# Four instead of three of eight units by seven products in the up and projection pairs

## What is computed

```python
h = h + 0.5 * swiglu(rms_norm(h, g1), w_gate1, w_up1, w_down1)      # FFN 1, inner width 5632
u = rms_norm(h, g_mix)
q, k, v, ... = split(u @ w_in)                                      # projection
merged = sigmoid(gate_A) * (attention(...) @ W_A) + sigmoid(gate_B) * (gla(...) @ W_B)
h = h + merged @ w_out
h = h + 0.5 * swiglu(rms_norm(h, g2), w_gate2, w_up2, w_down2)      # FFN 2
h = h + sigmoid(rms_norm(h, g_ple) @ w_ple_gate) * (p @ w_ple_proj)
return rms_norm(h, g_final)
swiglu(x, wg, wu, wd) = (silu(x @ wg) * (x @ wu)) @ wd
```

## Time and profile before

| what | us |
|---|---|
| median of three runs (2176.96 to 2177.33) | 2177.33 |
| the profiled execution | 2177.49 |
| its span, first to last instruction | 2175.8 |
| PE busy in it | 2161.8 |
| DVE busy in it | 1682.3 |
| ACT busy in it | 1150.2 |

### The profile page before, as it was taken

How to read it: one execution, slowest core, us unless ns; L and a number is a source line. 1 busy time by engine, 2 the same in 40 slices (tenths; PEclk the granted TensorE clock), 3 DMA queues, 4 the chain that set the end, 5 groups by cost and what they waited for, 6 DMA issues and landing times.

```text
span 2175.8 us, 24233 instructions
## 1 busy us (share of the span) xinstructions
PE 2161.8 (99%) x9760; PEld 1785.1 (82%) x9760; DVE 1682.3 (77%) x1750; ACT 1150.2 (53%) x1188; POOL 39.5 (2%) x71
## 2 busy tenths in 40 slices
PE   9999999999999999999999999999999999999998
PEld 7888888888888888878888888888888888888886
DVE  5898889988887877345666665889888998888755
ACT  6554555554455564455444554555555555455554
POOL 0000000000000000110100000000000000000000
PEclk9999999999999999999999999999999999999999
DMA  8655655565565655565665555655565565555464
GB/s 313 220 182 191 229 190 184 200 218 184 191 214 173 216 196 188 169 181 176 183 177 168 189 185 182 241 187 189 193 227 184 193 218 189 197 207 199 143 215 145
DMA packets 140752, 425.75 MB, mean 196 GB/s; under 512 B 10440, under 2 KB 10448, under 8 KB 126304
## 3 DMA queue, kind: packets, MB, share of 16 engines
q1 hardware_dynamic: 138592, 418.68, 57.3%
q0 software_dynamic: 1472, 4.70, 0.8%
q10 hardware_dynamic: 576, 0.82, 0.1%
HBM read 422.06 MB, written 2.11 MB: 195 GB/s over the span
## 4 chain that ended last, share of the span: by engine, by line
PE 93%; DVE 4%; issue 1%; ACT 1%; DMA 0%; SPq 0%; POOLq 0%; POOL 0%; DVEq 0%; ACTq 0%
PE acc L1669 11%; PE acc L1671 11%; PE acc L1670 11%; PE acc L1626 8%; PE acc L1628 8%; PE acc L1627 8%; PE turn L1669 6%; PE turn L1671 5%; PE turn L1670 5%; PE fox L1671 5%; PE fox L1669 5%; PE fox L1670 5%; DVE w_lo L1187 1%; PE turn L1646 1%; DVE raw_r L1187 1%
## 5 line engine op out<-in xcount | busy, mean ns | idle before, releaser
L1131 DVE TENSOR_TENSOR w_lo<-raw,w_hi 128x1024 fp32r<-128x1024 f32 x211 | 263.8, 1256 | 241.4 <-ACT w_hi L689 241.1
L689 ACT ACTIVATE w_hi<-raw 128x1024 fp32r<-128x1024 f32 x211 | 222.9, 1060 | 285.1 <-PE acc L1628 258.9
L1626 PE MATMUL acc<-w_hi,x_both 128*128 128x512 f32 x512 | 203.9, 398 | 0.0
L1628 PE MATMUL acc<-w_hi,x_both 128*128 128x512 f32 x512 | 199.8, 390 | 0.0
L1627 PE MATMUL acc<-w_lo,x_both 128*128 128x512 f32 x512 | 199.4, 389 | 0.0
L746 ACT ACTIVATE w_hi<-raw 128x2048 fp32r<-128x2048 f32 x61 | 117.1, 1921 | 86.4 <-PE fox L1671 22.8
L746 ACT ACTIVATE more_r<-lo_raw 128x2048 fp32r<-128x2048 f32 x63 | 120.5, 1920 | 74.3 <-DVE more L1201 37.1
L1187 DVE TENSOR_TENSOR raw_r<-raw,w_hi 128x2048 fp32r<-128x2048 f32 x61 | 139.3, 2286 | 17.1 <-ACT w_hi L746 16.7
L1187 DVE TENSOR_TENSOR w_lo<-lo_raw,more_r 128x2048 fp32r<-128x2048 f32 x63 | 143.7, 2286 | 10.1 <-ACT more_r L746 9.7
L746 ACT ACTIVATE more_r<-raw 128x2048 fp32r<-128x2048 f32 x55 | 105.3, 1919 | 67.1 <-DVE more L1201 33.3
L746 ACT ACTIVATE w_hi<-lo_raw 128x2048 fp32r<-128x2048 f32 x52 | 99.5, 1918 | 59.0 <-DVE more L1201 22.5
(11 more groups left out here) (501 smaller groups left out, 5540.9 us busy)
## 6 DMA issues: line engine op xcount, KB each, us to landing
lo_raw<-in_ffn_up SPq DMA_DIRECT2D x46, 1024.0 KB, 4.8
raw<-in_ffn_up SPq DMA_DIRECT2D x44, 1024.0 KB, 4.9
raw<-in_w_merge_gate SPq DMA_DIRECT2D x64, 512.0 KB
raw<-in_ffn_w_down SPq DMA_DIRECT2D x24, 1024.0 KB, 5.1
more<-in_ffn_up SPq DMA_DIRECT2D x21, 1024.0 KB, 4.9
lo_raw<-in_ffn_w_down SPq DMA_DIRECT2D x21, 1024.0 KB, 5.1
raw<-in_ffn_up SPq DMA_DIRECT2D x38, 512.0 KB, 3.8
raw<-in_w_in SPq DMA_DIRECT2D x36, 512.0 KB, 3.6
```

Of the source, the lines that this page charges most:

```text
L689: nc.scalar.activation(w_hi[:, slot, :, :], raw[:, slot, :, :], ACT.Copy).then_inc(hi_split, 1)
L1131: nc.vector.tensor_tensor(w_lo[:, slot, :, :], raw[:, slot, :, :], w_hi[:, slot, :, :].bitcast(F32), ALU.subtract).then_inc(lo_split, 1)
L1626: nc.tensor.matmul(to, hi(kt)[:, tok], w_hi[:, slot, k, :], start=kt == 0, stop=False)
L1628: last = nc.tensor.matmul(to, lo(kt)[:, tok], w_hi[:, slot, k, :], start=False, stop=kt == BK * nb - 1)
```

## The change

Four of eight units instead of three go by seven products, in every up pair but the first two of the first feed-forward and the first of the second, and in the projection's pairs 18 to 20. The down pairs stay at three of eight (two of six in the last part). The A units need a fourth small buffer and a fourth place for the token sums; both lie in a new tile `spare` of 5 x 512 elements a partition. The room for it comes from the descriptor ring of the transfers that POOL issues (`dynamic_dma_scratch_size=4096`). The sums of the tokens and their split run over as many steps as there are shared units. The last item of a list now counts up by what `item_counts` gives.

```diff
-US, HS = 3, 3
+US = {"up": 4, "mix": 4}
+TRIOS, HS = 4, 3
...
-    return down_shared(PAIR[ffn][i].part) if PAIR[ffn][i].kind == "down" else US
+    return down_shared(PAIR[ffn][i].part) if PAIR[ffn][i].kind == "down" else US[PAIR[ffn][i].kind]
...
-                    trio = min((t for t in range(US) if t not in held),
+                    trio = min((t for t in range(TRIOS) if t not in held),
...
+        spare, spare_r = shared(("spare", [P, 5, COLS], F32), ("spare_r", [P, 5, COLS], F32R))
...
+            if trio == 3:
+                return ((spare, spare_r)[split][:, 2:5, :],)
...
-        s_hi = room_r[:, 0:3, :].rearrange("p u (s c) -> p u s c", s=4)
-        s_lo = room_r[:, 3:6, :].rearrange("p u (s c) -> p u s c", s=4)
+        s_hi = [*[room_r[:, u, :] for u in range(3)], spare_r[:, 0, :]]
+        s_lo = [*[room_r[:, 3 + u, :] for u in range(3)], spare_r[:, 1, :]]
...
-                        if (n == 0 or i == LAST_DOWN + 1) and 3 <= k <= 5:
+                        if (n == 0 or i == LAST_DOWN + 1) and 0 <= k - 3 < shared_units(name, i + 1):
                             split_sums(name, i + 1, k - 3)
-                        if (n == 0 or i == LAST_DOWN + 1) and 2 <= k <= 4:
+                        if (n == 0 or i == LAST_DOWN + 1) and 0 <= k - 2 < shared_units(name, i + 1):
                             make_sums(name, i + 1, k - 2, hi, lo)
...
-                            last.then_inc(multiplied, 1)
+                            last.then_inc(multiplied, item_counts(name, it))
...
-    nc = bacc.Bacc("TRN2", target_bir_lowering=False, num_devices=1)
+    nc = bacc.Bacc("TRN2", target_bir_lowering=False, num_devices=1, dynamic_dma_scratch_size=4096)
```

More of the change, by code:

```diff
@@ L173, in item_tables @@
 def item_tables(block):
-    counts, steps, stages, after = {"raw": [0] * TALL, "trio": [0] * US}, 0, {}, {}
+    counts, steps, stages, after = {"raw": [0] * TALL, "trio": [0] * TRIOS}, 0, {}, {}
     for name, first in FIRST.items():
@@ L181, in item_tables @@
         slots = ring_order([i for i, kind in kinds if kind != "B"], TALL, 4 if name == "ffn1" else 0)
-        quad_free, trio_free = [b0 - 2, b0, early, early], [early] * US
+        quad_free, trio_free = [b0 - 2, b0, early, early], [early] * TRIOS
         raw_free, raw_split = [0, 0, b0 - 2, b0, early], [b0 - 2, b0, 0, 0, 0]
@@ L253, in sum_number @@
         downs = sum(down_shared(part) for part in range(len(PARTS)))
-        first = (US + downs + US) * (name == "ffn2")
+        first = (US["up"] + downs + US["mix"]) * (name == "ffn2")
         if PAIR[name][pair].kind == "up":
@@ L257, in sum_number @@
         if PAIR[name][pair].kind == "mix":
-            return first + US + downs + u
-        return first + US + sum(down_shared(n) for n in range(PAIR[name][pair].part)) + u
+            return first + US["up"] + downs + u
+        return first + US["up"] + sum(down_shared(n) for n in range(PAIR[name][pair].part)) + u
     x_tm = x[0].rearrange("(t p) d -> p t d", p=P)
@@ L367, in sums_of @@
         def sums_of(name, pair, u):
-            return (hid_hi[:, u], hid_lo[:, u]) if PAIR[name][pair].kind == "down" else (s_hi[:, u], s_lo[:, u])
+            if PAIR[name][pair].kind == "down":
+                return hid_hi[:, u], hid_lo[:, u]
+            return tuple(s[u].rearrange("p (s c) -> p s c", s=4) for s in (s_hi, s_lo))
         x_t = slab[:, SLABS - KD:, :, :].rearrange("p k t c -> p k (t c)")
@@ L400, in build @@
         tall_full = [sem(f"tall_full{i}") for i in range(TALL)]
-        trio_full = [sem(f"trio_full{i}") for i in range(US)]
+        trio_full = [sem(f"trio_full{i}") for i in range(TRIOS)]
         steps_made, parts_copied, combined = sem("steps_made"), sem("parts_copied"), sem("combined")
```

## The result

| | before | after |
|---|---|---|
| median, us | 2177.14 (2176.20 to 2177.33) | 2230.36 (2226.61 to 2234.12, 4 runs) |
| ratio | 1 | 1.0245, interval 1.0233 to 1.0257 |
| profiled execution, us | 2177.49 | 2234.12 |
| its span, us | 2175.8 | 2232.4 |

The changed kernel is slower by 53 us; the forecast was 2218 us, 41 more than before, with a range of 2200 to 2236. Direction and mechanism were right. The profiled execution is the slowest of the four and lies 16 us over the forecast.

The account below looks back on a forecast made before the run. It took VectorE's row of A units at the stage's end to bound up-to-up stages; 9.8 + 14.6 + 8.3 - 0.4 + 1.0 - 8.8 - 10.2 + 10.9 + 15.1 = +40.3 us on 2177.33 gave 2218 us, range 2200 to 2236.

Parts of the forecast that it names:

- VectorE's row of A units: End of stage: each A unit costs VectorE 4.85 us, TensorE 2.72; the fourth uses up VectorE's lead, so TensorE stalls.
- r + 1.68 + 4 x 4.85 + 6.91: Stage length: r from `combine` to B3's split, that split, four A units, TensorE's remainder; 45.6 us in pair 7.
- TensorE's saving: In 22 pairs a plain unit of 24 matmuls becomes 12 + 9: 66 matmuls fewer, 15.0 us.
- Stages that gain or only pay: Pairs 14 and 20 -10.2 us together, pairs 3 and 9 -8.8, pairs 5 and 11 +10.9.
- Edits costed at nothing: Loads, shorter descriptor ring, ScalarE's copies of new units and the last item's larger count: 0 us taken.
- the fourth rival: Halves of A units land late or ScalarE's order costs 1 us more in each of 15 stages: 2233 us, chance 0.08.
- third rival: Stalls lower TensorE's clock to 1.2 GHz for A2 and A3, 5.4 us more in nine stages: 2267 us, chance 0.05.
- VectorE's lead at `combine`: VectorE's wait at `combine` should fall to about 1 us in pairs 8 and 9 and stay over 2 after downs.

Follow-up runs that it names:

- the kernel with one step: The changed kernel with three of four step subtractions left out in up and projection pairs, tiles loaded instead, products not the reference's: 2163.42 us, ratio 0.9938.
- the kernel with spare matmuls: The changed kernel with 165 spare matmuls, results overwritten, ahead of A0 in eleven stages that stalled: 2222.12 us, ratio 1.0208.
- a better order of the waits: The changed kernel with the transposes' copies and VectorE's taking over moved behind the sixth unit of up-to-up stages, except pair 13: 2217.37 us, ratio 1.0185.
- the additional operation: The kernel before plus one unused VectorE reduction over 2048 elements in nine stages (pairs 1, 2, 7, 8, 13): 2199.52 us, ratio 1.0103.
- GpSimd's subtractions of two tiles: From the changed kernel with the step subtractions of A0 and A1 in up and projection pairs made by GpSimd: 2263.22 us, ratio 1.0399.

## Why the prediction was right, and where 12 us were missing

- **VectorE's row of A units sets the stage.** Right. TensorE stalls before A1 and A2 in the stages of pairs 2, 7, 8 and 13 and of the second feed-forward's pair 1, as forecast, with the sum r + 1.68 + 4 x 4.85 + 6.91 met in pair 7's stage to 0.3 us. (The stages of pairs 6, 12, 18 and 19 have one such stall and not two, and nine stages a short one before S6, which was not forecast.) Taking steps away gives TensorE's own time (2163.42); adding 2.28 us of VectorE's work to a stage of before costs nearly all of it.
- **TensorE's saving.** Right: 66 matmuls, 13.6 of the 15.0 us seen once VectorE is out of the way. The step from matmuls to time holds only in stages in which nothing else ends last.
- **Stages that gain or only pay.** Pair 14 (36.25 for 36.3), pairs 3 and 9 (40.06 for 40.2), pairs 5 and 11 (44.20 for 44.2): right.
- **Edits costed at nothing.** Right for the ring, by its own run, and for ScalarE, by the kernel with one step. The loads were right but for some late ones: in after VectorE waits eight times for the second half of an A unit's weights, 8.4 us in all (before: twice, 1.0 us). Four of these waits are in the stages of pairs 5 and 11, which kept the length that was forecast. The other four stand before A2's steps in the stages of pairs 6 and 12: 0.22, 0.31, 0.44 and, in the second feed-forward's pair 12, 1.64 us. These stages took 41.78, 41.91, 42.00 and 43.20 us where 41.4 was forecast; less the wait, all four are within 0.2 us of it. That is the fourth rival's mechanism, in four stages and not in 15, and over 1 us in one.

```profile
266.10 0.69 DVE L1204 TENSOR_TENSOR raw<-raw 128x512 f32<-128x512 f32 x1 [1.51 <-DMA room<-in_ffn_up]
...
303.13 0.69 DVE L1204 TENSOR_TENSOR lo_raw<-lo_raw 128x512 f32<-128x512 f32 x1 [0.22 <-DMA more<-in_ffn_up]
...
1956.43 0.69 DVE L1204 TENSOR_TENSOR lo_raw<-lo_raw 128x512 f32<-128x512 f32 x1 [1.64 <-DMA corner<-in_ffn_up]
```

- **The clock.** The mis-sized term. The forecast put the cost of falls at nothing, since no row of before showed one after its short stalls (0.23 us), and named them as its third rival, with 5.4 us in each of nine stages and a chance of 0.05. The falls came in seven stages and cost 1.2 to 1.7 us each, since TensorE was back at the full level before A2 had ended and A3 ran at full speed. The seven stages that kept their clock in the kernel with spare matmuls are 10.5 us shorter there, together; most of the 12 us between the two profiled executions (2234.12 and 2222.14).
- **The rest of the sum.** The spare-matmul kernel has no falls and is still 4 us above the forecast, 0.2 to 0.6 in each up-to-up stage of the feed-forwards and 0.1 or less in those of pairs 18 and 19. In pairs 6 and 12 a part of it is the late loads. In pair 7's stage 0.16 is r (17.76 for 17.6) and 0.14 the hand-over from the end of A2's split to TensorE's first matmul, which the forecast's start-to-start durations left out. The stages of pairs 8 and 13 were not taken apart in this way.
- **VectorE's lead at `combine`.** Half right. The wait fell to 49.6 us in all, from 73.3. The forecast named the wrong pairs for the fall: in front of the stages of pairs 8 and 9 before already had 0.56 and 0.90 us, and after has 0.39 and, behind a fall of the clock, 2.40. The wait did fall in front of pair 7's stage, from 3.28 to 0.81. It stayed over 2 in front of pairs 5 and 11, the second down pair of a part (2.2), as forecast, and behind the stages with a fall of the clock (2.4 to 2.5), which wasn't; for the up pair that follows the downs (6 and 12) it is 0.9 to 1.1, where over 2 was forecast.

That the runs of after differ by 7.5 us fits a number of falls that changes from one execution to the next. The mean granted clock of TensorE in the two slower runs (2234.12 and 2232.25 us) is 0.994, and in the two faster ones (2228.48 and 2226.61) 0.995 and 0.996. The stages of only one execution are on record, so where the falls lay in the others is not shown.

| stage, us | before | forecast | after | spare matmuls |
|---|---|---|---|---|
| pair 7 | 42.38 | 45.6 | 45.94 | 45.89 |
| pair 8 | 42.95 | 46.6 | 48.41 | 46.85 |
| pair 13 | 42.81 | 46.95 | 48.68 | 47.43 |

## What to carry to other kernels

Before moving work to an engine that looks partly idle, follow it through the stage from its last wait to the point where the other engine needs it. Idle time ahead of that wait can't be used: VectorE, with 3 to 6 us of idle per stage, had 0.1 to 0.5 to give. Such a change should be made pair by pair, where the stage table shows room, and not by kind. Where an engine is made to stall, look at what its clock does after the stall. And look for a better order of the waits (13 us here, falls of the clock included, for two lines) before looking for less work.

## What the runs showed of the hardware that was not expected

- Stalls of TensorE of under 2 us were followed by a fall of its granted clock to 1.2 GHz: in seven stages of after behind two stalls of 1.2 to 1.9 us each, and in before with the additional operation behind a single one of 1.85 us. Others of the same length were not (pair 2 of the first feed-forward in after, 46.82 us at 1.00; the 1.84 us in pair 8's stage with the additional operation). What decides between them stays open. Each fall in after cost 1.2 to 1.7 us.
- 165 spare matmuls, 37 us of work at 0.2267 us each, made the kernel 8 us faster: they ran where TensorE would have waited, and the clock stayed up.
- GpSimd's subtractions of two tiles and VectorE's take turns: 2.28 us became 3.3 to 3.4 on VectorE, 1.3 became up to 3.3 on GpSimd.
- A descriptor ring cut to 4096 bytes cost nothing that could be measured here (2177.02 against 2177.02).
